# First modulation in four column blocks, gates of the mixer by column groups, modulated rows on VectorE, first token numbers from rank

## The reference

```python
mod = silu(c) @ ada_w + ada_b                     # 6 x 1024 values per request
sh1, sc1, g1, sh2, sc2, g2 = split(mod, 6)
h = rms_norm(x, norm1_g) * (1 + sc1) + sh1        # the first modulation
proj = h @ w_in                                   # aq, ak, av, mq, mk, mv, mo, mg (16 gates), bg
# windowed attention with sinks; bidirectional mLSTM, whose gates come from mg
merged = bg_a * (attn @ w_up_attn) + bg_m * (mlstm_out @ w_up_mlstm)
x = x + g1 * (merged @ w_out)
h2 = rms_norm(x, norm2_g) * (1 + sc2) + sh2       # the second modulation
# router: best of 4 groups, best 2 of its 4 experts; each of 16 experts is a gated MLP
x = x + g2 * sum_e w_e * ((silu(h2 @ w_gate[e]) * (h2 @ w_up[e])) @ w_down[e])
y = rms_norm(x, final_norm_g)
```

## Time and profile before

| | us |
|---|---|
| median of 3 runs | 824.31 (824.17 to 826.28) |
| the profiled execution | 824.84 |
| its span, first to last instruction | 823.0 |
| PE busy, DVE busy, ACT busy, POOL busy | 709.9, 516.8, 398.5, 240.3 |
| granted TensorE clock, mean share of 2.4 GHz | 0.94 |

### The profile page before, as it was taken

One profiled execution on the slowest core, in us unless ns is written; L12 is line 12 of the kernel. 1 busy time (PEld: TensorE's weight loads), 2 busy tenths in 40 slices (PEclk: granted clock), 3 DMA queues, 4 the chain that ended last, 5 costly groups with the idle time before them and its releaser, 6 DMA issues.

```text
span 823.0 us, 9832 instructions
## 1 busy us (share of the span) xinstructions
PE 709.9 (86%) x3656; PEld 567.0 (69%) x3656; DVE 516.8 (63%) x618; ACT 398.5 (48%) x475; POOL 240.3 (29%) x123
## 2 busy tenths in 40 slices
PE   3679989989999999989988178999999999999820
PEld 2456767767788788877877167888878887877710
DVE  2445533550554446878128848888888888888627
ACT  4332312412727446324125157767777777766523
POOL 1233322433223133358545202222222232300030
PEclk9799999999999999999998579999999999999965
DMA  9994546456632122674701687999999999994353
GB/s 338 328 345 138 174 129 208 146 213 207 179 99 56 52 77 64 209 244 154 291 0 56 230 315 294 376 382 381 379 377 386 377 385 377 387 378 157 119 193 139
DMA packets 74495, 192.15 MB, mean 233 GB/s; under 512 B 14350, under 2 KB 47382, under 8 KB 68316
## 3 DMA queue, kind: packets, MB, share of 16 engines
q1 hardware_dynamic: 67076, 169.79, 58.7%
q0 software_dynamic: 4272, 11.31, 4.0%
q10 hardware_dynamic: 3112, 10.59, 3.2%
HBM read 179.04 MB, written 16.83 MB: 238 GB/s over the span
## 4 chain that ended last, share of the span: by engine, by line
PE 46%; DVE 23%; issue 14%; ACT 8%; DMA 5%; POOL 1%; ACTq 1%; POOLq 0%; SPq 0%; DVEq 0%
PE psum L801 37%; DVE moe_low L2126 11%; PE psum L876 3%; ACT half_high L1462 2%; ACT xbuf L1362 2%; PE psum L862 2%; DMA h_rows<-rot_pT 2%; ACT xbuf L1370 2%; DMA front_ring<-ada_w 1%; PE psum L1005 1%; DVE xbuf L1777 1%; DVE stat L1782 1%; DVE xsT_low L2135 1%; PE psum L1028 1%; DVE slots L1912 1%
## 5 line engine op out<-in xcount | busy, mean ns | idle before, releaser
L2245 POOL TENSOR_TENSOR low_ring<-front_ring,high_ring 128x1024 fp32r<-128x1024 f32 x54 | 131.4, 2436 | 254.3 <-ACT high_ring L1275 254.3
L1275 ACT ACTIVATE high_ring<-front_ring 128x1024 fp32r<-128x1024 f32 x54 | 57.0, 1056 | 194.3 <-PE psum L801 167.7
L801 PE MATMUL psum<-h_low,high_ring 128*128 128x512 f32 x312 | 118.9, 398 | 0.0
L2126 DVE TENSOR_TENSOR moe_low<-front_ring,half_high 128x2048 fp32r<-128x2048 f32 x48 | 107.9, 2286 | 10.4 <-ACT half_high L1462 10.4
L801 PE MATMUL psum<-h_high,low_ring 128*128 128x512 f32 x248 | 103.1, 416 | 11.8 <-DVE h_low L1661 10.8
L801 PE MATMUL psum<-half_high,xsT_low 128*128 128x512 f32 x256 | 103.6, 405 | 10.4 <-DVE xsT_low L2135 6.2
L801 PE MATMUL psum<-half_high,xsT_high 128*128 128x512 f32 x256 | 102.0, 398 | 0.0
L801 PE MATMUL psum<-moe_low,xsT_high 128*128 128x512 f32 x256 | 101.8, 398 | 0.0
L801 PE MATMUL psum<-h_high,high_ring 128*128 128x512 f32 x248 | 98.7, 398 | 0.0
L1462 ACT ACTIVATE half_high<-front_ring 128x2048 fp32r<-128x2048 f32 x48 | 90.9, 1914 | 8.6 <-PE psum L801 8.6
L2126 DVE TENSOR_TENSOR moe_low<-slots,half_high 128x2048 fp32r<-128x2048 f32 x32 | 73.1, 2288 | 13.0 <-ACT half_high L1462 13.0
(11 more groups left out here) (287 smaller groups left out, 1250.2 us busy)
## 6 DMA issues: line engine op xcount, KB each, us to landing
front_ring<-w_down SPq DMA_DIRECT2D x16, 2048.0 KB, 11.0
front_ring<-w_in SPq DMA_DIRECT2D x34, 512.0 KB, 5.1
xbuf<-ada_w SPq DMA_DIRECT2D x32, 512.0 KB, 4.1
slot<-w_gate SPq DMA_DIRECT2D x8, 2048.0 KB, 9.8
front_ring<-w_up SPq DMA_DIRECT2D x8, 2048.0 KB, 9.6
slots<-w_up SPq DMA_DIRECT2D x8, 2048.0 KB, 9.6
slots<-w_gate SPq DMA_DIRECT2D x8, 2048.0 KB, 10.0
y_rows<-inout ACTq DMA_DIRECT2D x16, 512.0 KB, 11.0
```

The lines of the kernel that those rows point to most:

```text
L801: mm = pe.matmul(out, lhs(a, k), rhs(b, k), start=(start and k == 0 and a == 1), stop=(stop and k == count - 1 and (a, b) == (0, 0)))
L1275: act.activation(dst, src.rearrange("p (k n) -> p k n", k=KD), ACT.Copy).then_inc(high_ready, 1)
L2126: dve.tensor_tensor(low_of(slot, h), half_of(slot, h), half_high[place].bitcast(F32), ALU.subtract).then_inc(low_dve, 1)
L2245: pool.tensor_tensor(low, src, high.bitcast(F32), ALU.subtract).then_inc(low_ready, 1)
```

## The change

Seven edits, in program order.

1. The first modulation is loaded and computed in four blocks of all 1024 input features by 2 x 256 columns. Block n gives sh1 and sc1 for k = 2n and 2n+1. Four weight pieces (ak, av, aq0, aq1) are loaded between the blocks and used beside them, each with split buffers of its own; their low parts and all low parts of h are written by DVE. POOL starts with the fifth piece.
2. The square roots of the first norm are taken per request, and silu of c is applied while c's transpose is copied out of PSUM.
3. The gates `mg` move ahead of `mq`, and are one unsplit product on four column groups (8 matmuls of 512 columns), copied to SBUF by DVE and added by one matmul with a constant (`sum`).
4. The ada pieces stand elsewhere in the list; their results alternate between banks 6 and 7, and the other projection results use banks 0 to 5, with mv and mo placed by hand. `tokens_out` waits for each bank just before it uses it.
5. The 4 MB of zeros for unused rows are stored after mk0 in place of after aq3.
6. DVE writes all four h2 rows, in its order after each rstd; ACT and POOL no longer take part. SP stores all four rows before it loads the next expert weights and the second gate rows.
7. Token numbers of the first 16 tiles (each expert's first tile) come from `rank` itself; those of the others follow later (`ids_more`). Counting tiles, weighing choices and the weights' last steps move between or behind the first expert's splits. Rows are gathered for tiles 2 and 3 without a copied index. x^T is emptied and split in two halves per tile.

```diff
-    pieces = [(f"ada{b}", j) for b in range(2) for j in range(KD)]
-    pieces += [("ak", 0), ("av", 0)]
+    pieces = [("ak", 0), ("av", 0), ("aq", 0), ("aq", 1)]
...
-    for name, beside in (("aq", (1, 1, 1, 1)), ("mq", (2, 1, 2, 1)), ("mk", (2, 1, 2, 1)),
-                         ("mv", (2, 2, 2, 2)), ("mo", (2, 2, 2, 2))):
-        pieces += [("mg", 0)] if name == "mv" else []
+    for name, beside in (("aq", (0, 0, 2, 2)), ("mq", (2, 2, 2, 2)), ("mk", (2, 2, 2, 1)),
+                         ("mv", (2, 2, 1, 1)), ("mo", (2, 2, 2, 1))):
+        pieces += [("mg", 0)] if name == "mq" else []
...
-BANK.update({name: 7 for name in PROJECTED if name.startswith("ada")})
-BANK.update({name: n % 7 for n, name in enumerate(n for n in PROJECTED if not n.startswith("ada"))})
+BANK.update({name: 6 + int(name[3:]) % 2 for name in PROJECTED if name.startswith("ada")})
+BANK.update({name: n % 6 for n, name in enumerate(n for n in PROJECTED if not n.startswith("ada"))})
+BANK.update({"turn4": 5, "gateT": 5, "mv0": 0, "mv1": 1, "mv2": 2, "mv3": 3,
+             "mo0": 4, "mo1": 6, "mo2": 0, "mo3": 1})
...
             load_first(0)
+            load_piece(("ak", 0))
             load_first(1)
-            for piece in (("ak", 0), ("av", 0)):
-                load_piece(piece)
+            load_piece(("av", 0))
+            load_piece(("aq", 0))
             load_first(2)
+            load_piece(("aq", 1))
             load_first(3)
...
-            for t in range(2):
-                sp.wait_ge(h2_pool, t + 1)
+            for t in range(TT):
+                sp.wait_ge(h2_dve, t + 1)
                 store_h2(t)
             wait_full(sp, "wo3.1")
             load_in(1, 1, GATE)
-            sp.wait_ge(hm_ready, TT)
-            spread_rows(3, g2b, gate2_landed)
-            for t in range(2, TT):
-                sp.wait_ge(h2_dve, t - 1)
-                store_h2(t)
             sp.wait_ge(xs_landed[1], 16)
             for q in range(2):
                 load_down(q, q)
+            sp.wait_ge(hm_ready, TT)
+            spread_rows(3, g2b, gate2_landed)
...
+            def gate_parts():
+                name, piece = "gate_parts", ("mg", 0)
...
+                for i in range(2):
+                    for g in range(4):
+                        k = 2 * g + i
+                        mm = pe.matmul(bank(name)[g * QUAD:(g + 1) * QUAD, :], raw_piece(piece)[:, 16 * k:16 * k + QUAD],
+                                       xT[:, k, :], start=(i == 0), stop=(i == 1))
...
+            columns_out(to_keys, range(0, 2))
+            first_block(1)
+            columns_out(to_values, range(0, 2))
+            turn_block(1)
+            columns_out(to_keys, range(2, 4))
+            columns_out(to_values, range(2, 4))
+            first_block(2)
+            columns_out(to_query0, range(0, 4))
+            turn_block(2)
+            columns_out(to_keys, range(4, 6))
+            columns_out(to_values, range(4, 6))
+            first_block(3)
+            columns_out(to_query0, range(4, 6))
+            turn_block(3)
+            columns_out(to_query1, range(0, 6))
+            for piece in FIRST_PIECES:
+                columns_out(piece, range(6, KD))
...
             add_x(0)
             add_x(1)
             rstd(0)
+            h2_rows_out(0)
             add_x(2)
             rstd(1)
+            h2_rows_out(1)
             logit_out(0)
             add_x(3)
             rstd(2)
             h2_rows_out(2)
...
             link(dve.tensor_reduce(rk, s8, AX.X, ALU.add))
+            places(rk)
...
+            wait_full(dve, "ids")
+            emptied(dve.tensor_scalar(ids[:, 0:N_EXP], bank("ids", N_EXP), float(2 * TOK), None, ALU.add))
...
             def split_x(s):
-                dve.wait_ge(xT_high, s + 1)
-                dve.tensor_tensor(xsT[1], psum[:, 3:5, :].rearrange("p b (k t) -> p (b k) t", k=4),
-                                  xsT[0].bitcast(F32), ALU.subtract).then_inc(xT_low, 1)
+                for b in range(2):
+                    dve.wait_ge(xT_high, s * 2 + (b + 1))
...
-            weigh_choices()
             low_half(0, 0, GATE, 0)
+            split_x(0)
             low_half(1, 1, GATE, 1)
-            split_x(0)
+            number_tiles()
             low_half(2, 2, UP, 0)
             low_half(3, 3, UP, 1)
-            finish_weights()
+            weigh_choices()
```

More of the change, by code:

```diff
@@ L336, in hybrid_layer @@
         vT = pTflat[:, 1024:1536]
+        first_split = [[ring[:, n, :] for ring in (high_ring, low_ring)] for n in range(2)]
+        for n, place in ((0, "og"), (1, "oT")):
+            first_split.append([placed_over(f"first_{part}{n}", place, i * PIECE, [P, PIECE])[:, :]
+                                for i, part in enumerate(("high", "low"))])
         acc = [pTflat[:, 1024 + n * 512:1536 + n * 512] for n in range(2)]
@@ L2170, in _ @@
             split_he(0)
+            finish_weights()
             def tile_step(s, q, stored, last=False):
@@ L2310, in _ @@
             gather(1, ids[:, 1:2])
+            for s in (2, 3):
+                pool.wait_ge(xT_full, s - 1)
+                gather(s % 2, ids[:, s:s + 1])
             def fetch(s, q):
@@ L2369, in shape_constants @@
     put(EARLY, early, "one", 1.0)
+    total = np.zeros((P, P), f)
+    for c in range(4 * M_HEADS):
+        total[c::QUAD, QUAD * (c // M_HEADS) + c % M_HEADS] = 1.0
+    put(EARLY, early, "sum", total)
     put(LATE, late, "tri", (i[:, None] < i[None, :]).astype(f))
```

516 lines of the change are left out of this document (267 added, 249 removed), and 2 rows, old and new, of the table ROUTER.

## The result

| | before | after |
|---|---|---|
| median of 20 runs each, us | 825.60 (820.88 to 828.90) | 820.44 (816.10 to 825.78) |
| ratio, 95% interval | | 0.9941 [0.9925, 0.9958] |
| profiled execution, its span, granted clock | 824.84, 823.0, 0.940 | 825.50, 823.5, 0.936 |

The kernel became 0.6% faster, not 2.5%: 820.4 us against a forecast of 804.5 and a range from 796 to 815.

What follows compares the result with a forecast made beforehand. PE was taken to set the pace in the experts, DMA close behind, with gains only where PE waits elsewhere. Start, projections, router and tiles: 824.84 - 3.9 - 8.0 - 9.6 + 1.2 = 804.5 us, range 796 to 815.

Steps and rivals of the forecast that it cites:

- The start: Work up to aq2: aq2 starts at 66.5 in place of 71.29, giving 3.9 us; bounds 7.8 and -2.
- the cycle's latency: In the start, block, copy, turn, scale, h and splits repeat three times; PE idles some 3.1 us after blocks 1 and 2.
- Rival C: The start gives nothing: DVE's one order stretches the cycle, all at the lower clock; 810.4 or 813.6 us, chance 0.16.
- The projections: Stage of projection products: 8.0 us faster, from mg and two removed waits less new waits and the zeros; bounds 4.5 and 11.7.
- The ada3 wait: In the projections, ada3 no longer shares ada2's bank, so 3.15 us idle and 1.6 of lower clock go: 4.8.
- The wait before mv0: In the projections, mv0 has conv7's bank, whose DVE instructions start when mk3 ends, so PE waits 1.9 us.
- The router: Router stage: ids release the gather 9.2 us earlier, PE's first expert product comes 9.6 us earlier; bounds 12 and 6.
- The tiles: Expert tiles: splitting x in two halves costs 0.1 us per tile, 1.2 in all; bounds -2 and +3.
- A: The clock stays up in the start and the two new bank waits don't occur: 797.4 us, chance 0.11.
- B: DMA takes over as the bound of the tiles; half the router's gain is given back: 809.3 us, chance 0.09.
- D: In the router a store or landing weight load still holds the gather; only DVE's 2.4 us remain: 811.7, chance 0.07.
- E: PE's wait for the split of x grows in each tile until the clock falls there: 832 us, chance 0.05.

Runs made afterwards that it cites:

- the first experiment: The kernel after, with the 4 MB store of zeros issued behind mq0's load in place of mk0's: 810.98 us, ratio to before 0.9827.
- the early ids alone: The kernel before with the router part, but h2 rows of tiles 0 and 1 on GpSimd and stores in their old order: 827.82 us, ratio 1.0023.

## Why the prediction was wrong

The direction was right, the size was not. Two sums in it are off by little and change nothing: the terms up to the first product add to 22.5 and not 22.6, and the lower bound of the projections is 4.8 and not 4.5. Point by point, in the prediction's order.

**The start, forecast -3.9, wrong by 6.8 us.** The forecast was aq2 at 66.5, of which 3.9 for the clock. With the gaps filled the start after is 67.23, against 62.6 forecast without the clock's share: 4.6 us of latency were missed. They are: 1.3 up to the first product (23.9 for 22.6; the 16 transposes took 3.65 and not 1.8, 0.23 each, where the next eight take 1.09 and the 32 of the earlier trace rows took 0.11 each); 1.8 for the low part of av, a wait that the forecast did not see, since I summed DVE's instructions without writing down their order against block 1; 1.4 behind the last product, where swap 0, the transposes of v and swap 1 take 3.64 and not 2.2, 1.32 of it for a raw copy on ACT that waits for the swap before it. The rest, 2.1, is the difference between that trace and after's profiled one, 6.0 us, where the sum had 3.9 for the clock: 4.6 lost behind the two gaps, and 1.5 ahead of them (x 0.3 later, blocks 0 and 1 slower by 0.9 and 0.6). So the term that failed most is the cycle's latency. Rival C had the outcome, a start that gives nothing, and in part the cause, DVE's one order; not every cycle was at the lower clock, and the start lost 2.9 us where C had 2. I gave it 0.16. That the loads do not bind was right: PE waited for no piece of weights before 73 us.

**The projections, forecast -8.0, measured +5 on the same count.** The step that failed is "the 4 MB of zeros, moved behind mk0, delay mk1's load by some 10 us that its lead of 13 nearly covers: 0.5". The delay of some 10 was right: against the first experiment mk1's load came 10.7 us later. The lead was read from the old order of the pieces; in the new one it was 2.9. So the term was 10.3 us in the trace and 9.5 in the median, not 0.5. The other terms held or were a little off. The ada3 wait is gone, as forecast. mg's products became 1.72 and 1.0 us of matmuls. The wait before mv0 is 1.94 us (1.9 forecast), that of the turn of ada4 1.39 (1.3). Behind the first the clock fell (7.32 for 24 products at 157.47), which stood in the bounds and not in the sum: 1.6. Without the zeros the stage lost only 2.7 us against the forecast: these 1.6, and 1.15 by which PE waits for a copy on ACT ahead of the first scores, which the forecast didn't have.

**The router, forecast -9.6, measured -9.5 between the two profiled executions.** Right in sum, by two errors that cancel: the gather was issued 34.7 us after the last piece of wo began and not 32.1 (1.6 of the 2.6 are products behind the wait for that piece that ran at the lower clock, which they didn't in before's trace; the rest lies behind them, in the chain of rows and logits), and from there to PE's first product it took 7.7 and not 10.3. The steps hold: ids bind after the change, the parts are worth little alone and much together. But a part of the 9.5 is the luck of the trace; like for like it is 7.4. The port lock of the Trainium skill ("SBUF — State Buffer", section "SBUF: two separate sides") is borne out by the same rows: with GpSimd's work gone, every h2 row of DVE takes 1.28 to 1.30 in after, where the one at 444.13 had taken 3.06. Where GpSimd kept its rows, with the early ids alone, the slow one is there again:

```profile
451.08 3.08 DVE L1970 SCALAR_TENSOR_TENSOR rot_pT<-xbuf,small,mqk 128x1024 f32<-128x1024 f32 x1
```

**The attention stage, forecast nothing, measured -0.2**, and -3.3 against the kernel before with its zeros moved (219.7 us and 223.0). That bank numbers change there "at no cost" was too little: a wait goes. In before, at the start of the out-projection:

```profile
390.93 0.47 PE L801 MATMUL psum<-high_ring,merged_low 128*128 128x512 f32 x1 [1.73 <-DVE mvb L1926]
```

All five kernels with the old code there show this wait of 1.73 us, and four of them products at the lower clock behind it, worth 1.6 us; the ten kernels with the new code show neither. The code says why: `tokens_out` waited for its four banks at once, and now waits for each just before it uses it (edit 4), so in after the first product starts at 398.61, ahead of DVE's last copy, which ends at 400.34. The new bank numbers alone wouldn't do it, since one of the four still belongs to that last copy. No experiment took this part alone.

**The tiles, forecast +1.2, measured +1.5 to 2.0.** Right, and 1.1 of it is the halves.

**The rivals.** A (the clock stays up, no new bank waits): both waits came. B (DMA takes over in the tiles): no; from tile 1 on the tiles lost 0.1 us each, not half of the router's gain. C: its outcome came in the start. D: no. E: no; the clock stayed at 1.00 from 509.5 to 696 us. But the wait that E starts from was misread: PE waited for the split of x 0.46 to 0.67 us at every other tile before, and not 0.2, and waits 0.43 to 0.66 at every tile after, with one piece in place of halves still 0.3 to 0.6. No rival had the zeros: their late load was a term of 0.5 us with no bound of its own, although its delay, 10 us, was written beside it. Had that one cover been priced as gone, as was done for the others, the range would have reached 825.

## What to carry to other kernels

A large store has no deadline, but everything behind it in its queue has: put it where the transfer engines are idle in the profile, or cut it to the size of the loads around it. The cover of a moved step must be read from the new order, since the order that moves it may be what uses up the cover. And where a chain of small steps leaves PE idle for 3 us, filling two such gaps with products that nobody reads made the kernel 5.6 us faster in one case and 7.0 in another (5.5 and 5.7 by the ratios to before). A filling that took 7.1 us where the gap was 2.2 made it 3.2 us slower.

## What the runs showed of the hardware

- The clock after an idle stretch is not the same from run to run. The gap of 2.97 us behind the turn of block 1 was followed by products every 0.43 us in after (granted clock 0.77 from 22.7 to 60 us) and one of 2.96 by products every 0.23 in the first experiment (0.91), with the same code in the start. Behind the wait of 2.40 us near 366 the granted clock was 1.00 in before and 0.88 in the same kernel with its zeros moved, and the last tile differs in the same way. aq2 came between 68.94 and 73.26 in four kernels with the same start, so one profiled execution is no base for terms of 1 or 2 us.
- One request of 4 MB took 17.7 us to land, and a 512 KB load issued 9.5 us behind it in the same queue took 12.5; the same load took 5.3 in the first experiment, where the store stood elsewhere.
- Matmuls of 32 columns into four column groups in turn overlap: 32 records took 3.11 us, and 7.09 when all went to one group (granted clock 1.00 in both).
- PE's first matmuls are slow although the granted clock reads 1.00: after's 16 transposes at 13.51 took 0.23 us each (granted clock 1.00 from 13.5 to 17.1) and the next eight, at 19.86, 0.14; block 0 took 2.82 us and blocks 2 and 3 2.10 and 2.05. Before shows it too: its first 32 records of ada took 3.43 us and the next 32 1.93.
